# A two-block sequence model on one core: x and the parameter vectors arrive with channels over the partitions

## The chip, the cores and the metric

The kernel runs on one core of one Trainium2 chip. The metric is the device time of one execution in microseconds (us). Three timed runs of the kernel before gave 2650.94, 2653.60 and 2653.69 us, median 2653.6 us. One further execution was recorded by the profiler; its own time is 2655.73 us and its span, first to last instruction, 2653.9 us.

## The reference, cut to what matters

Two blocks follow each other on an array x of 1024 tokens by 1024 channels, all in float32. Only the beginning of the first block and its first residual are touched by the change:

```python
def rms_norm(x, g):
    y = xf * lax.rsqrt(jnp.mean(xf * xf, axis=-1, keepdims=True) + EPS)
    return (y * g.astype(jnp.float32)).astype(x.dtype)

h = rms_norm(x, g_mix[l])
z = jnp.einsum("bsd,de->bse", h, w_in[l]) + b_in[l]
va, ga, xb, gb, sa, sb = jnp.split(z, cuts, axis=-1)
...   # a convolution branch, a gated linear recurrence branch, their mixture m
x = x + jnp.einsum("bsd,de->bse", m, w_o[l])
h = rms_norm(x, g_mlp[l])
f = jnp.square(jax.nn.relu(jnp.einsum("bsd,df->bsf", h, w_1[l])))
x = x + jnp.einsum("bsf,fd->bsd", f, w_2[l])
```

Behind it come the second block (pooling, attention to a memory, a chunked matrix LSTM) and a last norm.

## The kernel before, in words

**Layout.** Inside the kernel every activation has its channels over the 128 partitions and its tokens along the free dimension: 8 tiles of 128 channels by 1024 tokens. A tile is worked on in two halves of 512 tokens ("half 0", "half 1"), and a half of a tile fills one PSUM bank. x itself comes from memory with tokens over the partitions (x_in, 8 tiles of 128 tokens by 1024 channels).

**Products.** A float32 product is made of three matmuls on values split in a high and a low part (three_products, L535 to L537: hi x hi, hi x lo, lo x hi). One weight block is 1024 rows by 128 output columns, 512 KB. For each half, block_product runs over 8 row tiles with three matmuls each, 24 in all, each 512 columns wide. The weight blocks have numbers in the order of use. Each is loaded by SyncE into one of 2 raw buffers, split by ScalarE (whi<-raw, L903) and VectorE (wlo<-raw, L1422) into one of 3 pairs of buffers; a split of block i waits until block i - 3 has been used for both halves ("used"), a load of block i until block i - 2 has been split. `ahead(k)` in an engine's program stands where it does this work up to block k.

**Order.** Every engine has its own program, written out by hand, which it runs strictly in order; points (names such as ("xb", 0, 0, 1)) join them by semaphores. PSUM banks go round in a ring of 8.

**The front.** SyncE loads the identity, four x tiles, block 0, the first group of parameter vectors, four x tiles, block 1, and the other three parameter groups; the 19 parameter vectors come as rows of 128 values. ScalarE squares each token tile with a running sum along the channels (x_squares, L923), takes the root; VectorE scales x by the factor (x_scales, L1464); TensorE transposes x (turn_x, L587) and the parameter rows (turn_rows, L566). Each transposed half tile is split from PSUM with the gain g_mix: high part by ScalarE (L912), low part by VectorE (L1437). TensorE's order is: parameter group 0; x half 0; blocks ("xb", 0, 0) and ("gb", 0, 0) on half 0; x half 1; parameter groups 1 to 3; block ("gb", 0, 1) on half 0; the same three blocks (called FIRST) on half 1, one after the other; then the block ("xb", 0, 1), and so on through the whole projection.

**The later stages that matter.** Three groups of recurrence gates with convolutions on VectorE (57 to some 525 us), then the 31-tap convolution on VectorE beside TensorE's projections (to 914 us), a layer norm, the product w_a_out, and from 1049 us the product with w_o, called "wo": 8 blocks by 2 halves.

**The residual before.** For each half of a "wo" tile, SyncE loads the piece of x with tokens over the partitions (xcols, L464), and TensorE adds it into the same bank by four matmuls of 128 columns against the identity (L678), behind the product's 24. ScalarE copies the bank out as x1 (L1119) and splits the high part for the next product; VectorE makes the low part and the sum of squares.

Of the kernel before, what the change touches and what calls it, by code (L numbers as in the profile page):

```python
# [6 lines left out]
ALU = mybir.AluOpType  # L7
ACT = mybir.ActivationFunctionType

P = 128  # L10
# [109 lines left out]
def build_program(nc, A, out):  # L120
    ctx = ExitStack()
    with ctx:
# [141 lines left out]
        x_rows = A["x"].rearrange("b (t p) d -> p (b t) d", p=P)  # L264
        x_in = sb("x_in", "y", 0, [P, NT, D])
        square_out = sb("square_out", "g", 32 * KB, [P, D])
        rows_in = [sb(f"rows_in{i}", "g", 36 * KB + 512 * i, [P, P]) for i in range(4)]
        row_pieces = [[] for _ in range(4)]
        for name, rows in PARAMS:
            a = A[name]  # L270
            flat_rows = a.rearrange("l (k p) -> (l k) p", p=P) if len(a.shape) == 2 else (
                a.rearrange("(k p) -> k p", p=P) if len(a.shape) == 1 else a.rearrange("l t (k p) -> (l t k) p", p=P))
            done = 0
            while done < rows:
                r = offsets[name] + done
                n = min(rows - done, P - r % P)
                row_pieces[r // P].append((rows_in[r // P][r % P:r % P + n, :], flat_rows[done:done + n, :]))
                done += n
# [35 lines left out]
        xcols = [sb(f"xcols{n}", "g", 64 * KB + 2048 * n, [P, NT // 2, P]) for n in range(2)]  # L314
# [75 lines left out]
        landings = ([f"rows{s}" for s in range(4)] + [f"x{t}" for t in range(NT)] + ["raw0", "raw1"]  # L390
# [9 lines left out]
        def sync(sp):  # L400
# [20 lines left out]
            def load_rows(s):  # L421
                for n, (dst, src) in enumerate(row_pieces[s]):
                    point = [("rows", s)] if n == len(row_pieces[s]) - 1 else []
                    sp.dma_start(dst, src).then_inc(*landed(f"rows{s}", *point))

            def load_x(t):
                sp.dma_start(x_in[:, t, :], x_rows[:, t, :]).then_inc(*landed(f"x{t}", ("x_in", t)))
# [16 lines left out]
            for t in range(NT // 2, NT):  # L444
                load_x(t)
            ahead(0)
            for s in range(1, 4):
                load_rows(s)
# [7 lines left out]
            for j in range(DT):  # L456
                ahead(number["wo", j] + 2)
                for half in range(2):
                    if j:
                        w.wait_ge(*at("x1_sum", j - 1, half))  # L460
# [3 lines left out]
                    sp.dma_start(xcols[half][:], x_rows[:, half * 4:half * 4 + 4, j * P:(j + 1) * P]).then_inc(  # L464
                        *landed(f"xc{half}", ("xcols", j, half)))
# [56 lines left out]
        def tensor(pe):  # L522
# [39 lines left out]
            def turn_rows(s):  # L562
                b = bank("rows", s)
                w.wait_ge(*at("rows", s))
                w.wait_ge(*at("ident"))
                pe.transpose(b[:, 0:P], rows_in[s][:], ident[:]).then_inc(*up("pe_done", ("rows_turned", s)))  # L566

# [13 lines left out]
            def turn_x(half):  # L581
                for j in range(DT):
                    b = bank("x", j, half)
                    for q in range(4):
                        t = half * 4 + q
                        w.wait_ge(*at("normed", t))
                        turned = pe.transpose(b[:, q * P:(q + 1) * P], x_in[:, t, j * P:(j + 1) * P], ident[:])  # L587
                    turned.then_inc(*up("pe_done", ("x", j, half)))
# [13 lines left out]


            turn_rows(0)
            turn_x(0)
            for key in FIRST[:2]:
                block_product(number[key], (*key, 0), h, "h", 0, used=False)
            turn_x(1)
            for s in range(1, 4):
                turn_rows(s)  # L610
            block_product(number[FIRST[2]], (*FIRST[2], 0), h, "h", 0, used=False)
            for key in FIRST:
                block_product(number[key], (*key, 1), h, "h", 1)
# [59 lines left out]
            for j in range(DT):  # L673
                for half in range(2):
                    b = block_product(number["wo", j], ("wo", j, half), mx, "mx", half, stop=False, used=half == 1)
                    w.wait_ge(*at("xcols", j, half))
                    for q in range(4):
                        last = pe.matmul(b[:, q * P:(q + 1) * P], xcols[half][:, q, :], ident[:], start=False, stop=q == 3,  # L678
                                         skip_group_check=True)
                    last.then_inc(*up("pe_done", ("x1_sum", j, half)))  # L680
# [210 lines left out]
        def scalar(act):  # L891
# [27 lines left out]
            def x_squares(half):  # L919
                for t in range(half * 4, half * 4 + 4):  # L920
                    w.wait_ge(*at("x_in", t))
                    w.wait_ge(*now("act_done"))
                    act.activation(square_out[:], x_in[:, t, :], ACT.Square, accum_out=stat[:, t:t + 1]).then_inc(*did(("x_square", t)))  # L923
                root(slice(half * 4, half * 4 + 4), f"x{half}")

            def h_tiles(half):
                for j in range(DT):
                    w.wait_ge(*at("x", j, half))
                    w.wait_ge(*at("par", 0))
                    split_hi(("h_hi", j, half), h[0][j][:, cut(half)], bank("x", j, half)[:], C("g_mix", j))  # L930

            w.wait_ge(*at("ones"))
            act.activation(square_out[:, 0:8], ones[:], ACT.Sqrt).then_inc(*did(("table",)))
# [87 lines left out]

            xb_tile(0, 0, [0])
# [91 lines left out]
            for j in range(DT):  # L1114
                ahead(number["wo", j] + 2)
                for half in range(2):
                    w.wait_ge(*at("x1_sum", j, half))
                    w.wait_ge(*at("mx_lo", j, 0))
                    act.activation(x1[j][:, cut(half)], bank("wo", j, half)[:], ACT.Copy).then_inc(  # L1119
                        *did(("x1", j, half), ("free", "wo", j, half)))  # L1120
                    w.wait_ge(*now("act_done"))
# [16 lines left out]
            for f in range(FC):  # L1138
                for j in range(DT):
# [5 lines left out]
                    for half in range(2):  # L1145
                        t = tmp[half]
                        w.wait_ge(*at("relu", f, j, half))
                        act.activation(t[:], t[:], ACT.Square).then_inc(*did(("relu_square", f, j, half)))  # L1148
                        w.wait_ge(*now("act_done"))
                        w.wait_ge(*(at("w2", f - 1, DT - 1, 1) if f else at("x1_sum", DT - 1, 1)))  # L1150
                        split_hi(("ff_hi", f, j, half), ff[0][j][:, cut(half)], t[:])
# [258 lines left out]
        def vector(dve):  # L1410
# [36 lines left out]
            def turn_rows(s):  # L1447
                block = slice(s * P, (s + 1) * P)
                w.wait_ge(*at("rows_turned", s))
                dve.tensor_copy(par[:, block], bank("rows", s)[:, 0:P]).then_inc(*did(("free", "rows", s)))  # L1450
                own()
                dve.tensor_scalar(parh[:, block], par[:, block], 0.5, None, ALU.mult).then_inc(*did(("par", s)))

# [3 lines left out]
            def x_scales(half):  # L1457
                columns = slice(half * 4, half * 4 + 4)
                w.wait_ge(*at("x_square", half * 4 + 3))
                mean(columns, f"x{half}")  # L1460
                inverse(columns, f"x{half}")
                own()
                for t in range(half * 4, half * 4 + 4):
                    dve.tensor_scalar(x_in[:, t, :], x_in[:, t, :], stat[:, t:t + 1], None, ALU.mult).then_inc(*did(("normed", t)))  # L1464

            def h_tiles(half):
                for j in range(DT):
                    w.wait_ge(*at("h_hi", j, half))
                    scaled_lo(("h_lo", j, half), h[1][j][:, cut(half)], bank("x", j, half)[:], C("g_mix", j), h[0][j][:, cut(half)],
                              ("free", "x", j, half))  # L1470

            x_scales(0)
            turn_rows(0)
            ahead(0)
            h_tiles(0)
            ahead(1)
            dve.memset(xb_in[:, 0:PAD_B], 0.0).then_inc(*did(("xb_pad",)))
            x_scales(1)
            ahead(2)
            h_tiles(1)  # L1480
            for s in range(1, 4):
                turn_rows(s)
# [624 lines left out]
        def gpsimd(pool):  # L2107
            w = Once(pool)
            w.wait_ge(*at("x", DT - 1, 1))
# [40 lines left out]
```

## Time and profile before

| | |
|---|---|
| median of three runs | 2653.6 us |
| the profiled execution's own time | 2655.73 us |
| its span | 2653.9 us |
| TensorE, matmuls | 2493.1 us busy, 94% |
| VectorE | 1413.2 us busy, 53% |
| ScalarE | 810.3 us busy, 31% |
| DMA, mean share of the 16 engines | 17.0% |
| mean granted TensorE clock | 0.971 of 2.4 GHz |

How to read it: the busy times are those of one execution on the chip. PE is TensorE's matmuls, PEld its weight loads (they overlap), DVE is VectorE, ACT ScalarE, POOL GpSimd, SP SyncE. A float32 matmul that is not split leaves two records. Matmuls are pipelined, so the distance from one start to the next tells more than the duration of one. PEclk is the granted clock as a share of 2.4 GHz; the first record of it is a rise at 19.9 us, and windows ahead of that show 1.00 without one.

### The profile page before, as it was taken

How to read it: one execution, taken by the hardware profiler on the slowest of the kernel's cores; microseconds unless marked ns; L12 is line 12 of the kernel's file. 1: busy time of each engine (PE TensorE's matmuls, PEld its weight loads, DVE VectorE, ACT ScalarE, POOL GpSimd, SP SyncE). 2: the span in 40 equal slices, each digit the busy share in tenths (PEclk: the TensorE clock that was granted, in tenths of full speed). 3: DMA queues.
4: the chain of work that ended last, by engine and by line, in shares of the span. 5: the costliest groups of instructions: out<-in, count | busy, mean ns of one | idle time of the engine just before them, and what ended most of it. 6: DMA issues, size and time to landing. Idle time of an engine off the chain costs nothing.

```text
span 2653.9 us, 26240 instructions
## 1 busy us (share of the span) xinstructions
PE 2493.1 (94%) x11144; PEld 2015.3 (76%) x11144; DVE 1413.2 (53%) x1699; ACT 810.3 (31%) x1202; POOL 2.8 (0%) x7
## 2 busy tenths in 40 slices
PE   8999999999999469999999999999789999999678
PEld 6686867788888148888888888887678777878577
DVE  5665665598899974243232232334665333631365
ACT  5435252512121152332022130232332231221354
POOL 0000000000000000000000000000000000000000
PEclk9999999999999789999999999999799999999889
DMA  4010202011111002211111111121111111111401
GB/s 133 27 56 27 64 12 70 20 55 48 48 48 48 16 15 61 83 49 55 48 48 48 48 48 53 46 69 40 50 46 56 38 33 48 40 48 55 128 22 59
DMA packets 224951, 133.15 MB, mean 50 GB/s; under 512 B 12730, under 2 KB 220858, under 8 KB 224834
## 3 DMA queue, kind: packets, MB, share of 16 engines
q1 hardware_dynamic: 224834, 131.47, 17.0%
q8 instruction: 88, 1.44, 0.2%
q14 instruction: 29, 0.24, 0.0%
HBM read 125.12 MB, written 6.32 MB: 50 GB/s over the span
## 4 chain that ended last, share of the span: by engine, by line
PE 81%; DVE 12%; ACT 4%; issue 1%; DMA 1%; SPq 1%; ACTq 0%; DVEq 0%
PE bank L535 24%; PE bank L537 24%; PE bank L536 24%; DVE uc L1559 4%; PE bank L599 4%; DVE sa L1559 2%; DVE wlo L1422 1%; PE bank L569 1%; DVE u_in L1559 1%; PE bank L770 1%; PE bank L786 1%; PE bank L678 1%; DVE uc L1676 0%; DVE tmp L1799 0%; PE bank L875 0%
## 5 line engine op out<-in xcount | busy, mean ns | idle before, releaser
L535 PE MATMUL bank<-h_hi,whi 128*128 128x512 f32 x2000 | 787.3, 394 | 3.6 <-issue 3.3
L537 PE MATMUL bank<-h_hi,wlo 128*128 128x512 f32 x2000 | 780.7, 390 | 0.0
L536 PE MATMUL bank<-h_lo,whi 128*128 128x512 f32 x2000 | 780.4, 390 | 0.0
L535 PEld LDWEIGHTS bank<-h_hi,whi 128*128 128x128 f32 x2000 | 376.7, 188 | 84.3 <-issue 5.6
L536 PEld LDWEIGHTS bank<-h_lo,whi 128*128 128x128 f32 x2000 | 376.7, 188 | 80.3 <-issue 2.9
L537 PEld LDWEIGHTS bank<-h_hi,wlo 128*128 128x128 f32 x2000 | 376.5, 188 | 78.7
L903 ACT ACTIVATE whi<-raw 128x1024 fp32r<-128x1024 f32 (+2 forms) x212 | 216.8, 1023 | 448.6 <-PE bank L537 446.6
L1422 DVE TENSOR_TENSOR wlo<-raw,whi 128x1024 fp32r<-128x1024 f32 (+2 forms) x212 | 251.4, 1186 | 163.5 <-ACT whi L903 161.8
L1559 DVE SCALAR_TENSOR_TENSOR uc<-u_in,par,uc 128x1024 f32<-128x1024 f32 x163 | 205.5, 1281 | 1.1
L537 PE MATMUL bank<-ff_hi,wlo 128*128 128x512 f32 x512 | 199.4, 389 | 0.0
L536 PE MATMUL bank<-ff_lo,whi 128*128 128x512 f32 x512 | 199.4, 389 | 0.0
L535 PE MATMUL bank<-ff_hi,whi 128*128 128x512 f32 x512 | 199.4, 389 | 0.0
L1770 DVE TENSOR_TENSOR x<-x,bank 128x512 f32<-128x512 f32 x64 | 44.0, 688 | 229.8 <-PE bank L537 229.8
L536 PEld LDWEIGHTS bank<-ff_lo,whi 128*128 128x128 f32 x512 | 96.2, 188 | 19.9
L535 PEld LDWEIGHTS bank<-ff_hi,whi 128*128 128x128 f32 x512 | 96.1, 188 | 19.9
L537 PEld LDWEIGHTS bank<-ff_hi,wlo 128*128 128x128 f32 x512 | 96.1, 188 | 19.9
L1148 ACT ACTIVATE tmp<-tmp 128x512 f32<-128x512 f32 x64 | 40.5, 632 | 227.4 <-DVE tmp L1759 227.4
L1759 DVE SCALAR_TENSOR_TENSOR tmp<-bank,factor 128x512 f32<-128x512 f32 x64 | 44.2, 691 | 115.9 <-PE bank L537 115.9
L599 PE MATMUL bank<-v,gate_w 128*128 128x512 f32 x224 | 97.5, 592 | 0.0
L1434 DVE TENSOR_TENSOR ff_lo<-tmp,ff_hi 128x512 fp32r<-128x512 f32 x64 | 44.3, 693 | 87.2 <-ACT ff_hi L912 87.2
L599 PEld LDWEIGHTS bank<-v,gate_w 128*128 128x128 f32 x224 | 42.6, 190 | 50.4 <-issue 48.3
L537 PE MATMUL bank<-vg_hi,wlo 128*128 128x512 f32 x192 | 75.9, 395 | 0.0
(341 smaller groups left out, 3075.5 us busy)
## 6 DMA issues: line engine op xcount, KB each, us to landing
raw<-in_w_in SPq DMA_DIRECT2D x92, 512.0 KB, 3.6
raw<-in_w SPq DMA_DIRECT2D x64, 512.0 KB, 3.8
raw<-in_w_b_out SPq DMA_DIRECT2D x16, 384.0 KB, 3.0
raw<-in_w_out SPq DMA_DIRECT2D x11, 512.0 KB, 3.4
x_in<-in_x SPq DMA_DIRECT2D x8, 512.0 KB, 5.5
raw<-in_w_a_out SPq DMA_DIRECT2D x8, 512.0 KB, 3.8
raw<-in_w_o SPq DMA_DIRECT2D x8, 512.0 KB, 3.5
xcols<-in_x SPq DMA_DIRECT2D x16, 256.0 KB, 2.8
```

The source lines that it names most:

```text
L535: pe.matmul(target, lh, rh, start=start, stop=False, skip_group_check=True)
L536: pe.matmul(target, lh, rl, start=False, stop=False, skip_group_check=True)
L537: last = pe.matmul(target, ll, rh, start=False, stop=stop and point is not None, skip_group_check=True)
L569: pe.matmul(b[:], ones_sq[:], data, start=j == 0, stop=j == DT - 1, skip_group_check=True).then_inc(*up("pe_done", point))
L599: last = pe.matmul(b[:], gate_w[n][:, PAIRS.index((a, c)), :], v[a][:, cut(half)], start=m == 0, stop=m == len(rows_) - 1)
L903: act.activation(hi, raw_, ACT.Copy).then_inc(*up("w_hi_done", ("w_hi", i)))
L1148: act.activation(t[:], t[:], ACT.Square).then_inc(*did(("relu_square", f, j, half)))
L1422: dve.tensor_tensor(lo, raw_, hi.bitcast(F32), ALU.subtract).then_inc(*up("w_lo_done", ("w", i)))
L1434: dve.tensor_tensor(lo, value, hi.bitcast(F32), ALU.subtract).then_inc(*did(name, *more))
L1559: dve.scalar_tensor_tensor(to, source, weight, to, ALU.mult, ALU.add).then_inc(*did(*point))
L1759: dve.scalar_tensor_tensor(t[:], b[:], 0.0, factor[:, cut(half)], ALU.max, ALU.mult).then_inc(*did(("relu", f, j, half), ("free", "w1", f, ...
L1770: dve.tensor_tensor(x1[j][:, cut(half)], x1[j][:, cut(half)], b[:], ALU.add).then_inc(*did(("x1_add", f, j, half), ("free", "w2", f, j, ha ...
```

## The change

- The host passes x transposed (x_t, channels by tokens) and all parameter vectors in one array of 128 by 512 (par). x_in is loaded as 8 pieces of two channel tiles by 512 tokens; par by one DMA. The loads of rows, their transposes and the transposes of x are gone.
- The mean square of a token is now a sum over partitions. ScalarE squares each channel half tile into one of four buffers x_sq; TensorE multiplies it, 128 tokens at a time, as the stationary operand with one column of ones and adds over the 8 tiles in one bank (x_sums); VectorE, ScalarE and VectorE make the factor from 4 columns; TensorE spreads it over the partitions (x_spread, 4 matmuls of 128 columns). VectorE multiplies x by gain and factor into one of four buffers x_z, ScalarE makes the high part, VectorE the low part, one tile behind.
- Blocks of FIRST are run abreast, tile by tile, in two or three banks (blocks_together): the first two on half 0, the third on half 0, all three on half 1.
- VectorE splits blocks 0 and 1 ahead of the h tiles.
- In "wo" the identity matmuls and ScalarE's copy are gone. VectorE adds the bank and xcols, which is now loaded with channels over the partitions, into x1.
- GpSimd's clearing of the gate weights no longer waits for the transposes.

```diff
-            for t in range(NT // 2):
-                load_x(t)
-            ahead(-1)
-            load_rows(0)
...
+            for j in range(0, DT, 2):
+                load_x(0, j)
             sp.dma_start(ident[:], A["ident"]).then_inc(*landed("ident", ("ident",)))
+            sp.dma_start(par[:], A["par"]).then_inc(*landed("par", ("par_in",)))
             ahead(0)
+            for j in range(0, DT, 2):
+                load_x(1, j)
...
+            def x_sums(half):
+                b = bank("x_sums", half)
+                for j in range(DT):
+                    w.wait_ge(*at("x_square", j, half))
+                    for q in range(4):
+                        last = pe.matmul(b[:, q:q + 1], x_sq[j % 4][:, q * P:(q + 1) * P], ones[:, 0:1], start=(j, q) == (0, 0), stop=j == DT - 1,
+                                         skip_group_check=True)
+                    last.then_inc(*up("pe_done", ("x_sum", j, half)))
+
+            def x_spread(half):
+                w.wait_ge(*at("ident"))
+                w.wait_ge(*at(f"x{half}"))
+                spread(0, half, "x_scale")
+
+            def blocks_together(keys, half):
+                together = [bank(*key, half) for key in keys]
+                for n in range(DT):
+                    w.wait_ge(*at("h_lo", n, half))
+                    for key, b in zip(keys, together):
...
+                        point = [(*key, half)] + ([("used", k)] if half else []) if n == DT - 1 else None
+                        three_products(...)
...
+            x_sums(0)
+            x_spread(0)
+            blocks_together(FIRST[:2], 0)
+            x_sums(1)
+            x_spread(1)
+            blocks_together(FIRST[2:], 0)
+            blocks_together(FIRST, 1)
             for t in range(1, GT):
                 block(("xb", 0, t), h, "h")
...
-                    b = block_product(number["wo", j], ("wo", j, half), mx, "mx", half, stop=False, used=half == 1)
-                    w.wait_ge(*at("xcols", j, half))
-                    for q in range(4):
-                        last = pe.matmul(b[:, q * P:(q + 1) * P], xcols[half][:, q, :], ident[:], start=False, stop=q == 3,
-                                         skip_group_check=True)
+                    block_product(number["wo", j], ("wo", j, half), mx, "mx", half, used=half == 1)
...
 # ScalarE
+                for j in range(DT):
+                    w.wait_ge(*at("x_in", j // 2 * 2, half))
+                    if half or j >= 4:
+                        w.wait_ge(*(at("x_sum", j - 4, half) if j >= 4 else at("x_sum", j + 4, 0)))
+                    act.activation(x_sq[j % 4][:], x_in[:, j, cut(half)], ACT.Square).then_inc(*did(("x_square", j, half)))
...
             x_squares(0)
             ahead(0)
+            root(slice(0, 4), "x0")
+            ahead(1)
             h_tiles(0)
-            ahead(1)
             x_squares(1)
+            root(slice(4, 8), "x1")
             ahead(2)
 # VectorE
+            w.wait_ge(*at("par_in"))
+            dve.tensor_scalar(parh[:], par[:], 0.5, None, ALU.mult).then_inc(*did(("par",)))
+            x_factors(0)
             ahead(0)
+            ahead(1)
             h_tiles(0)
...
+            x_factors(1)
             ahead(2)
             h_tiles(1)
...
+                    w.wait_ge(*at("wo", j, half))
+                    w.wait_ge(*at("xcols", j, half))
+                    dve.tensor_tensor(x1[j][:, cut(half)], bank("wo", j, half)[:], xcols[half][:], ALU.add).then_inc(
+                        *did(("x1", j, half), ("free", "wo", j, half)))
                     w.wait_ge(*at("h2_hi", j, half))
```

## Rows read from the trace of the kernel before

**Rows 1.** The page, part 1: busy us, share of the span, instructions.

```profile
PE 2493.1 (94%) x11144; PEld 2015.3 (76%) x11144; DVE 1413.2 (53%) x1699; ACT 810.3 (31%) x1202; POOL 2.8 (0%) x7
```

**Rows 2.** Windows: stretch and its length, busy us (instructions) of PE, PEld, DVE, ACT, POOL, PEclk, DMA.

```profile
57.00:877.00 820.00, 820.00 (x3374) 633.92 (x3373) 610.83 (x620) 270.50 (x321) 0.00 (x0) 1.00 0.15 44
...
600.00:700.00 100.00, 100.00 (x443) 82.87 (x442) 85.86 (x80) 20.83 (x27) 0.00 (x0) 1.00 0.18 53
```

**Rows 3.** Timeline of the front: start us, us, what, [idle before and its releaser].

```profile
5.34 1.06 ACT L923 ACTIVATE square_out<-x_in 128x1024 f32<-128x1024 f32 x1 [3.11 <-DMA x_in<-in_x]
10.75 0.17 DVE L1441 TENSOR_SCALAR stat<-stat 128x4 f32<-128x4 f32 x1 [9.72 <-ACT square_out L923]
11.41 0.75 DVE L1464 TENSOR_SCALAR x_in<-x_in,stat 128x1024 f32<-128x1024 f32 x1
12.37 0.47 PE L566 MATMUL bank<-ident,rows_in 128*128 128x128 f32 x1 [12.37 <-DMA rows_in<-in_lam]
14.21 6.15 PE L587 MATMUL bank<-ident,x_in 128*128 128x128 f32 x29 [0.19 <-DVE x_in L1464]
20.11 0.47 PE L535 MATMUL bank<-h_hi,whi 128*128 128x512 f32 x1
31.11 3.65 PE L587 MATMUL bank<-ident,x_in 128*128 128x128 f32 x32
35.39 0.50 PE L535 MATMUL bank<-h_hi,whi 128*128 128x512 f32 x1 [0.29 <-DVE h_lo L1437]
57.28 0.39 PE L535 MATMUL bank<-h_hi,whi 128*128 128x512 f32 x1
```

**Rows 4.** ScalarE's drain of "wo" (first and last start us), and the identity matmuls' timeline.

```profile
L1119 ACT ACTIVATE x<-bank x16: 597/597/597, 1056.1 to 1151.3; 128x512 f32<-128x512 f32 x16
...
1055.05 1.05 PE L678 MATMUL bank<-ident,xcols 128*128 128x128 f32 x8
```

**Rows 5.** An add from PSUM (the page, part 5), and one half's work in "wo".

```profile
L1770 DVE TENSOR_TENSOR x<-x,bank 128x512 f32<-128x512 f32 x64 | 44.0, 688 | 229.8 <-PE bank L537 229.8
...
1139.27 0.72 ACT L912 ACTIVATE h_hi<-x,par 128x512 fp32r<-128x512 f32 x1
1140.03 0.75 DVE L1437 SCALAR_TENSOR_TENSOR h_lo<-x,par,h_hi 128x512 fp32r<-128x512 f32 x1 [4.99 <-ACT h_hi L912]
```

**Rows 6.** One-column matmuls: windows of L687 and what follows it; timeline of L849.

```profile
1862.90:1869.70 6.80, 6.80 (x32) 6.80 (x33) 0.00 (x0) 0.00 (x0) 0.00 (x0) 0.50 0.00 0
1869.70:1873.30 3.60, 3.60 (x18) 3.60 (x19) 2.13 (x9) 1.37 (x3) 0.00 (x0) 0.50 0.02 5
...
2497.46 0.95 PE L849 MATMUL bank<-ones,kts 128*128 128x1 f32 x8
```

**Rows 7.** A square, a scaled z, its high and low part (128x512 each), later in the kernel.

```profile
L1148 ACT ACTIVATE tmp<-tmp 128x512 f32<-128x512 f32 x64 | 40.5, 632 | 227.4 <-DVE tmp L1759 227.4
...
1895.66 0.63 ACT L912 ACTIVATE h_hi<-tmp 128x512 fp32r<-128x512 f32 x1 [1.42 <-DVE tmp L1799]
1896.33 0.69 DVE L1434 TENSOR_TENSOR h_lo<-tmp,h_hi 128x512 fp32r<-128x512 f32 x1 [0.69 <-ACT h_hi L912]
1896.93 0.74 DVE L1799 SCALAR_TENSOR_TENSOR tmp<-x,small,bank 128x512 f32<-128x512 f32 x1
```

**Rows 8.** Timeline of block 3's split, and the work behind it on VectorE.

```profile
47.19 1.05 ACT L903 ACTIVATE whi<-raw 128x1024 fp32r<-128x1024 f32 x1
48.27 1.23 DVE L1422 TENSOR_TENSOR wlo<-raw,whi 128x1024 fp32r<-128x1024 f32 x1 [8.92 <-ACT whi L903]
49.41 0.81 DVE L1495 TENSOR_SCALAR v<-xb_in,par 128x1024 f32<-128x1024 f32 x1
```

**Rows 9.** Products after idle time: timeline at 944 us, and windows around 1900 us.

```profile
945.13 0.63 PE L536 MATMUL bank<-un_lo,whi 128*128 128x512 f32 x1
945.55 0.63 PE L537 MATMUL bank<-un_hi,wlo 128*128 128x512 f32 x1
...
1907.00:1910.90 3.90, 0.60 (x4) 0.54 (x4) 2.92 (x4) 1.58 (x3) 0.00 (x0) 1.00 0.00 0
```

More of the change, by code:

```diff
@@ L261, in weight_views @@
                     wlo[k % 3][:, 0:n].rearrange("p (k c) -> p k c", k=kt))
[L264 to L278, printed above, removed]
+        x_t = A["x_t"].rearrange("(j p) t -> p j t", p=P)
+        x_in = sb("x_in", "y", 0, [P, DT, SEQ])
+        x_sq = [sb(f"x_sq{n}", "g", 48 * KB + 2048 * n, [P, HALF]) for n in range(4)]
+        x_z = [sb(f"x_z{n}", "g", 56 * KB + 2048 * n, [P, HALF]) for n in range(4)]
         h = pair("h", "h", 0, DT)
@@ L313, in build_program @@
         x1 = [sb(f"x1_{j}", "y", 4096 * j, [P, SEQ]) for j in range(DT)]
-        xcols = [sb(f"xcols{n}", "g", 64 * KB + 2048 * n, [P, NT // 2, P]) for n in range(2)]
+        xcols = [sb(f"xcols{n}", "g", 64 * KB + 2048 * n, [P, HALF]) for n in range(2)]
         squares = [sb(f"squares{n}", "g", 68 * KB + 2048 * n, [P, HALF]) for n in range(2)]
@@ L388, in build_program @@
         add_keys = {"yb": GT, "ob": NH, "oc": NH}
-        landings = ([f"rows{s}" for s in range(4)] + [f"x{t}" for t in range(NT)] + ["raw0", "raw1"]
+        landings = (["par"] + [f"x{half}_{j}" for half in range(2) for j in range(0, DT, 2)] + ["raw0", "raw1"]
                     + ["ident", "mask", "gate0", "gate1", "xc0", "xc1", "mem", "bias", "rcnt", "row_out", "mp", "last", "gain"]
@@ L419, in ahead, with load_x @@
                         sp.dma_start(view[:, :, c0:c1], src).then_inc(*landed(f"raw{i % 2}", *point))
[L421 to L427, printed above, removed]
+            def load_x(half, j):
+                sp.dma_start(x_in[:, j:j + 2, cut(half)], x_t[:, j:j + 2, cut(half)]).then_inc(*landed(f"x{half}_{j}", ("x_in", j, half)))
             def load_gates(g):
@@ L459, in sync @@
                     if j:
-                        w.wait_ge(*at("x1_sum", j - 1, half))
+                        w.wait_ge(*at("x1", j - 1, half))
                     else:
@@ L463, in sync @@
                         w.wait_ge(*at("mixed", DT - 1, 1))
[L464 removed]
+                    sp.dma_start(xcols[half][:], x_t[:, j, cut(half)]).then_inc(
                         *landed(f"xc{half}", ("xcols", j, half)))
@@ L919, in x_squares @@
             def x_squares(half):
[L920 to L924, printed above, removed]
+                for j in range(DT):
[3 more added lines that the diff above has]
+                    act.activation(x_sq[j % 4][:], x_in[:, j, cut(half)], ACT.Square).then_inc(*did(("x_square", j, half)))
             def h_tiles(half):
                 for j in range(DT):
-                    w.wait_ge(*at("x", j, half))
-                    w.wait_ge(*at("par", 0))
-                    split_hi(("h_hi", j, half), h[0][j][:, cut(half)], bank("x", j, half)[:], C("g_mix", j))
+                    w.wait_ge(*at("x_z", j, half))
+                    split_hi(("h_hi", j, half), h[0][j][:, cut(half)], x_z[j % 4][:])
             w.wait_ge(*at("ones"))
-            act.activation(square_out[:, 0:8], ones[:], ACT.Sqrt).then_inc(*did(("table",)))
+            act.activation(small[:, 0:8], ones[:], ACT.Sqrt).then_inc(*did(("table",)))
             x_squares(0)
             ahead(0)
+            root(slice(0, 4), "x0")
+            ahead(1)
             h_tiles(0)
-            ahead(1)
             x_squares(1)
+            root(slice(4, 8), "x1")
             ahead(2)
@@ L1116, in scalar @@
                 for half in range(2):
[L1117 to L1121, printed above, removed]
+                    w.wait_ge(*at("x1", j, half))
                     w.wait_ge(*at("ya", DT - 1, 1))
@@ L1445, in inverse @@
                 dve.reciprocal(stat[:, columns], stat[:, columns]).then_inc(*did((name,)))
[L1447 to L1452, printed above, removed]
             dve.memset(ones[:], 1.0).then_inc(*did())
@@ L1456, in vector, with x_factors @@
             dve.memset(ones_sq[:], 1.0).then_inc(*did(("ones",)))
-            def x_scales(half):
+            def x_factors(half):
                 columns = slice(half * 4, half * 4 + 4)
-                w.wait_ge(*at("x_square", half * 4 + 3))
-                mean(columns, f"x{half}")
+                w.wait_ge(*at("x_sum", DT - 1, half))
+                dve.tensor_scalar(stat[:, columns], bank("x_sums", half)[:, 0:4], 1.0 / D, EPS, ALU.mult, ALU.add).then_inc(
+                    *did((f"x{half}_mean",), ("free", "x_sums", half)))
@@ L1461, in x_scales @@
                 inverse(columns, f"x{half}")
[L1462 to L1470, printed above, removed]
@@ L1472, in vector, with h_tiles @@
-            x_scales(0)
-            turn_rows(0)
+            def h_tiles(half, follow=()):
+                b = bank("x_scale", half)
+                w.wait_ge(*at("x_scale", half))
+                for j in range(DT + 1):
+                    if j < DT:
+                        if half or j >= 4:
+                            w.wait_ge(*(at("h_lo", j - 4, half) if j >= 4 else at("h_lo", j + 4, 0)))
+                        dve.scalar_tensor_tensor(x_z[j % 4][:], x_in[:, j, cut(half)], C("g_mix", j), b[:], ALU.mult, ALU.mult).then_inc(
+                            *did(("x_z", j, half), *([("free", "x_scale", half)] if j == DT - 1 else [])))
+                    if j:
+                        w.wait_ge(*at("h_hi", j - 1, half))
+                        split_lo(("h_lo", j - 1, half), h[1][j - 1][:, cut(half)], x_z[(j - 1) % 4][:], h[0][j - 1][:, cut(half)])
@@ L2141 @@
                  "rcnt": rcnt}
+    inputs = {name: np.asarray(a, np.float32) for name, a in inputs.items()}
+    columns = [inputs.pop(name).reshape(-1, P) for name, _ in PARAMS]
+    constants["par"] = np.concatenate(columns).T
+    constants["x_t"] = inputs.pop("x").reshape(SEQ, D).T
     for name, a in [*inputs.items(), *constants.items()]:
```

38 lines of the change are left out of this document (6 added, 32 removed).

## The prediction, made before the changed kernel was run

> **What bounds the kernel now.** I read the page's busy times first, then windows over the stages, then the timeline of the first 60 us and of the residual at 1055 us. On the page the reader sees TensorE at 94% of the span and VectorE at 53% [rows 1]. The windows show TensorE full from 57 to 877 us, with VectorE at 74% over all of it and 86% from 600 to 700 us, its convolution [rows 2]. So VectorE still has gaps there, where it waits for TensorE's blocks, so a delay of TensorE in the first 57 us is carried on into VectorE's late stretch and to the end, one for one. In the first 57 us the timeline shows three stretches of products: the first from 20.11 us, ended by 31.1 us, the rest from 35.39 us; the block ("xb", 0, 1) starts at 57.28 us, and from there TensorE is never short of work [rows 3]. That start is my first mark. The second is the output product of the mixer, "wo": its 16 drains start from 1056.1 to 1151.3 us, so a half tile takes (1151.3 - 1056.1) / 15 = 6.35 us, all of it TensorE's [rows 4].
>
> **The residual ("wo").** Four float32 matmuls against the identity stand behind each product. They leave 8 records, 8 x 0.112 = 0.9 us [rows 4]. The product itself is 24 matmuls at 0.227 us (in the front 96 such matmuls go from 35.39 to 57.28, the first of them slow [rows 3]), 5.44 us. Sum 6.35, as measured. Taken away 16 times: 16 x 0.91 = 14.5 us gained. In their place VectorE adds x from PSUM, nearest row 0.69 us for the same shape [rows 5], and ScalarE no longer copies. VectorE's part of a half is then 0.69, a wait of 0.72 for ScalarE's split, 0.75 for the lo part, some 0.69 for the square total [rows 5], and a weight split of 1.22 every second half: under 4.1 us of 5.44. Queued behind the new wait are only that half's own operations. At the end of the stage the up-projection needs the last half 5.44 us after it was produced; add, split and lo part take 2.2 us. So the edit costs nothing elsewhere; if VectorE's part did become the bound it would be worth the lost cover, at most 14.5 us. The x tiles are asked for one tile ahead (10.9 us) as before.
>
> **The front: what goes.** 64 transposes of x: 32 of them before 20.1 us at about 0.21 us, 32 after 31.11 us in 3.65 us; the parameter transposes, 8 scalings of x on VectorE (0.75 us) and 22 small loads. None of the loads ended a wait but the first.
>
> **The front: the sums of squares.** With channels on the partitions the mean is over partitions, so x_sums issues 8 x 4 float32 matmuls of one column for each half. The same kind stands in the trace (L687, 16 matmuls, 32 records): 32 records in 6.8 us, 0.213 us each at a granted clock of 0.50, that is 1.2 GHz [rows 6]. At 2.4 GHz the same kind took 8 records in 0.95 us with the drain, 0.112 us each [rows 6]. So a half is 64 records: 64 x 0.213 = 13.6 us at 1.2 GHz, 64 x 0.112 = 7.2 us at 2.4 GHz. These are the ends; I take 13.6 us for half 0, since TensorE comes from idle.
> The Trainium skill ("TensorE: Matmul & The Clock Gate", section "LDWEIGHTS (loading the stationary operand)") gives a weight load as its columns over 1.2 GHz, 107 ns for 128, with no word of the array's clock. By it a half of sums would be 64 x 0.107 = 6.8 us whichever clock is granted. The trace agrees at the high clock (0.112) and not at the low one (0.213), so the sum does not use it.
> Does this work raise the clock? The window from 1862.9 to 1869.7 us is nothing but such matmuls, TensorE busy all of it, and the clock stayed 0.50; the window behind it, 3.6 us of 256-column products, still shows 0.50, and only then it rose [rows 6]. I take it that it does not raise it.
>
> **Half 0, in us.** First x tile used 5.34 [rows 3]; ScalarE squares a 512 piece in 0.63 [rows 7]; TensorE starts the sums at about 5.7, is slower (1.7 a tile) than squares and loads, and ends at 19.4. Mean, root, reciprocal: 0.25 wait and 0.66 (10.75 to 11.41 [rows 3]): 20.2. VectorE now splits blocks 0 and 1 first, 2 x 1.15 (48.27 to 49.41 [rows 8]): 22.5; the spread over TensorE, 8 x 0.213 = 1.7, is beside it. Then per tile z on VectorE (0.74), hi on ScalarE (0.63), lo on VectorE (0.69) [rows 7]; as lo runs one tile behind z, VectorE's pace is 0.67 + 0.60 = 1.27, and the first lo is ready at 24.6. Products start at 24.7 instead of 20.11. Two blocks abreast need 6 x 0.227 = 1.36 per tile, just over VectorE's pace: 10.9 us. But TensorE has idled about 2.7 us behind the slow spread and starts at 1.2 GHz. Other starts from idle show the price: 512 columns take 0.43 instead of 0.23 [rows 9], and the clock is back after 3.6 us of products (1869.7 to 1873.3) or 7.5 us (12.4 to 19.9, transposes) [rows 3, 6]. Lost is 1 - 0.227/0.427 = 47% of that time, 1.7 to 3.5; I take 5 us, 2.4. Ends: 24.7 + 10.9 + 2.4 = 38.0. Before: 31.1.
>
> **Half 1.** The sums wait in TensorE's queue behind those products. After a pause the granted clock held for some 3.9 us and then fell (1907.0 to 1910.9) [rows 9]: 3.5 us of sums at 0.112 (31 records), 33 at 0.213: 10.5 us (ends 7.2 and 13.6). 48.5. Factor, 0.9: 49.4. Block 2's split follows on ScalarE and VectorE (1.05 and 1.22, ScalarE's part beginning with the reciprocal): 51.6; the spread is beside it. Before, TensorE was here at 35.39. Then 96 matmuls x 0.227 = 21.8, as before, plus 2.4 for the low clock: 75.8. VectorE's tiles, done by 65, don't hold this up.
>
> **A wait that is added.** The three blocks run abreast to the last tile, so all three weight buffers come free only at the end; block 3's hi split waits for the first of them. Behind it: ScalarE copies xb half 1 (0.59), splits hi (1.05), VectorE lo (1.23) [rows 8], beginning 1.2 us before TensorE ends: ("xb", 0, 1) starts 1.8 us late, at 77.6. Before, block 3 was split at 47.19 to 49.5, 8 us ahead. VectorE's convolution and GELU stand 7 us later against TensorE than before; its idle time before the gates takes that up.
>
> **Sum.** Front 77.6 - 57.3 = 20.3 lost, residual 14.5 gained: +5.8 us. On the profiled execution's own 2655.7 us that is 2661.5; that execution lay 2.1 us above the median of the runs, 2653.6, so the prediction is 2659.4 us. The parameter load of 256 KB, POOL's clearing moved to the start and the halved parameters (one VectorE operation) lie in VectorE's idle time before 19 us; without that cover they would be about 1 us.
>
> **Rivals.**
> (a) One-column matmuls do raise and hold the clock, ends on the faster side. Sums of half 0: 35 records at 0.213, then 29 at 0.112, end 16.4; factor 17.2, splits 19.5, products 21.7 to 32.6 at full clock; sums 7.2 to 39.8; 40.6; block 2 at 42.7; 64.5; 66.3. Front 9.0 lost, net -5.5, 2648.1 us. For it: TensorE's queue is full all the time. Against it: [rows 6]. It decides from where the front loses less than 14.5 us. Chance 0.20.
> By the skill's load time the front would come out close to this too.
> (b) The low clock lasts longer everywhere: sums of half 1 all at 0.213 (+3.1), each restart 7.5 us (+1.1 twice): net +11.1, 2664.7 us. For it: the start at 12.4 us took that long [rows 3]. Against it: the products at 1869.7 us took 3.6 [rows 6]. Chance 0.12.
> (c) The residual gives nothing, because VectorE's add becomes late: +20.3, 2673.9 us. Against it: 1.3 us and more to spare in each half. Chance 0.03. That a loss before 57 us is absorbed by VectorE's late stretch, net -14.5, has 0.02.
> The forecast has 0.63, its own range 2656 to 2663.
>
> **How the numbers follow.** A measurement of this kernel can tell about 0.2%, 5.3 us: slower begins at 2658.9, just under the forecast, faster at 2648.3. Slower: 0.58 of the forecast's 0.63, (b), (c): 0.52. Faster: a third of (a), and 0.02: 0.09. The rest, 0.39, is no change. The range 2648 to 2667 takes in (a) and (b).
>
> **What would show it.** "wo" drains every 5.44 us, its identity matmuls gone: else the 14.5 is wrong. x_sums of half 0 in 13.6 us at 0.213, of half 1 in 7.2 to 13.6; first product at 24.7; first matmuls at 0.43; ("xb", 0, 1) at 77.6 with TensorE idle 1.8 us ahead of it. If the sums run at 0.112, (a) holds. If TensorE has gaps after 80 us that it had not, a consumer is late and the sum lacks a term.

## The result, and the profile of the changed kernel

The changed kernel takes 2657.28 us against 2652.61 us before (medians of 20 runs each, taken side by side): ratio 1.0019, 95% interval 1.0013 to 1.0026. It is 4.7 us, 0.2%, slower. Forecast were 5.8 us more and 2659.4 us. One of the changed kernel's 20 runs was a slow one, 13480.1 us; nothing here explains it, the interval is worked out without it, and it does not move the median.

The first view is the timeline of the front of the changed kernel. Line numbers have moved: L561 is x_sums, L551 the spread, L516 to L518 the three products, L886 and L1403 the high and the low part of a weight block.

```profile
4.20 1.15 ACT L907 ACTIVATE x_sq<-x_in 128x512 f32<-128x512 f32 x2 [1.96 <-DMA x_in<-in_x_t]
4.88 13.82 PE L561 MATMUL bank<-ones,x_sq 128*128 128x1 f32 x64 [4.88 <-ACT x_sq L907]
19.16 0.18 DVE L1426 RECIPROCAL stat<-stat 128x4 f32<-128x4 f32 x1 [0.27 <-ACT stat L899]
19.26 2.33 DVE L1403 TENSOR_TENSOR wlo<-raw,whi 128x1024 fp32r<-128x1024 f32 x2
21.57 1.41 DVE L1445 SCALAR_TENSOR_TENSOR x_z<-x_in,par,bank 128x512 f32<-128x512 f32 x2
23.77 0.79 PE L516 MATMUL bank<-h_hi,whi 128*128 128x512 f32 x1 [2.23 <-DVE h_lo L1415]
...
36.27 9.71 PE L561 MATMUL bank<-ones,x_sq 128*128 128x1 f32 x64
48.67 0.79 PE L516 MATMUL bank<-h_hi,whi 128*128 128x512 f32 x1
...
72.05 1.23 DVE L1403 TENSOR_TENSOR wlo<-raw,whi 128x1024 fp32r<-128x1024 f32 x1 [12.77 <-ACT whi L886]
73.42 0.47 PE L516 MATMUL bank<-h_hi,whi 128*128 128x512 f32 x1 [1.72 <-DVE wlo L1403]
```

The reader sees the two blocks of 64 records that replaced the transposes, 13.8 and 9.7 us long, and that VectorE has two weight splits to do behind the first before it can touch a tile. Against [rows 3] the first product comes at 23.77 instead of 20.11 us, the second stretch at 48.67 instead of 35.39, and the block ("xb", 0, 1) at 73.42 instead of 57.28: 16.1 us lost.

Between half 1's sums and the product at 48.67 lie 2.7 us, in which TensorE has only the spread to do:

```profile
46.32 1.04 ACT L886 ACTIVATE whi<-raw 128x1024 fp32r<-128x1024 f32 x1
46.68 2.08 PE L551 MATMUL bank<-ident,stat 128*128 128x128 f32 x8 [0.71 <-DVE stat L1426]
47.39 1.23 DVE L1403 TENSOR_TENSOR wlo<-raw,whi 128x1024 fp32r<-128x1024 f32 x1 [0.77 <-ACT whi L886]
```

That product, block ("gb", 0, 1) on half 0, needs nothing of half 1. It stands behind half 1's sums and spread in TensorE's program, and it waits for the split of its weights, which ScalarE and VectorE have behind half 1's root and factor, though the block's load was issued at 20.5 us. No run put the split or the product ahead, so what this order costs is not shown.

The second view is the residual stage: VectorE's add from the bank, with the start of the first and the last of the 16.

```profile
L1700 DVE TENSOR_TENSOR x<-bank,xcols x16: 691/692/692, 1070.8 to 1152.4; 128x512 f32<-128x512 f32 x16
```

(1152.4 - 1070.8) / 15 = 5.44 us for a half, where [rows 4] has 6.35: 16 x 0.91 = 14.5 us gained. VectorE waits for TensorE ahead of every add, 0.5 and 3.2 us ahead of the first two and then 1.3 and 2.6 us in turn, so it has room:

```profile
1147.00 0.69 DVE L1700 TENSOR_TENSOR x<-bank,xcols 128x512 f32<-128x512 f32 x1 [1.26 <-PE bank L518]
1152.44 0.69 DVE L1700 TENSOR_TENSOR x<-bank,xcols 128x512 f32<-128x512 f32 x1 [2.60 <-PE bank L518]
```

The third view is TensorE's waits from 57 to 900 us in the changed kernel (us in total, times, longest). There are two: the weight split, and 0.6 us in the gates of the recurrence, for VectorE. The kernel before has none in this stretch.

```profile
PE bank L516 <- DVE wlo L1403: 1.7, 1, 1.7
PE bank L590 <- DVE lru L1496: 0.6, 1, 0.6
```

The last view is windows of the changed kernel over half 1's sums and the products behind them (columns as in [rows 2]; the last but two is the granted clock).

```profile
36.30:40.60 4.30, 4.30 (x41) 4.30 (x39) 0.00 (x0) 2.52 (x4) 0.00 (x0) 1.00 0.00 0
40.60:46.00 5.40, 5.37 (x26) 5.29 (x25) 0.00 (x0) 0.00 (x0) 0.00 (x0) 0.50 0.00 0
46.70:50.80 4.10, 4.10 (x13) 3.50 (x14) 3.19 (x4) 3.01 (x5) 0.00 (x0) 0.50 0.20 56
```

The clock fell 4.3 us into the one-column matmuls although TensorE was busy with them all the time (about 0.11 us each ahead of the fall, 0.21 behind it), and the spread and the first products ran at 1.2 GHz.

In the two profiled executions themselves the spans differ by 0.7 us only (2653.9 and 2654.6). The front is 16.1 us late, TensorE's end before the layer norm 17.1 (877.3 and 894.3), and "wo" gives 14.5 back. Another 1.5 us comes back between 944 and 1049 us, from where the low clock of 1.2 GHz lies in these two executions: behind TensorE's last wait for the normed tiles it lasted 5.8 us before (980.15 to 985.9) and 2.4 us in the changed kernel (997.24 to 999.7). The 0.4 us that is left I can't place.

### The profile page after: what moved, and what is told of

Its sections match the earlier page's. It is cut to its first block, busy times and chain, and to the rows that moved or that the text cites. A ratio compares the mean times of both kernels' runs of the same rounds, so it can differ in the third digit from the quotient of the medians.

```text
span 2654.6 us, 26124 instructions
## 1 busy us (share of the span) xinstructions
PE 2497.7 (94%) x11092; PEld 2017.9 (76%) x11092; DVE 1426.8 (54%) x1716; ACT 800.7 (30%) x1186; POOL 2.8 (0%) x7
## 4 chain that ended last, share of the span: by engine, by line
PE 79%; DVE 14%; ACT 5%; issue 1%; DMA 1%; SPq 1%; ACTq 0%; DVEq 0%
PE bank L516 24%; PE bank L518 24%; PE bank L517 24%; DVE uc L1537 4%; PE bank L590 3%; DVE sa L1537 2%; DVE wlo L1403 1%; PE bank L561 1%; PE bank L544 1%; DVE u_in L1537 1%; PE bank L753 1%; PE bank L769 1%; ACT whi L886 0%; DVE tmp L1781 0%; DVE uc L1654 0%
## 5 line engine op out<-in xcount | busy, mean ns | idle before, releaser
L516 PE MATMUL bank<-h_hi,whi 128*128 128x512 f32 x2000 | 786.8, 393 | 6.7 <-issue 2.7
L518 PE MATMUL bank<-h_hi,wlo 128*128 128x512 f32 x2000 | 779.6, 390 | 0.0
L516 PEld LDWEIGHTS bank<-h_hi,whi 128*128 128x128 f32 x2000 | 376.5, 188 | 88.3 <-issue 5.0
L518 PEld LDWEIGHTS bank<-h_hi,wlo 128*128 128x128 f32 x2000 | 376.3, 188 | 78.7
L886 ACT ACTIVATE whi<-raw 128x1024 fp32r<-128x1024 f32 (+2 forms) x212 | 216.7, 1022 | 446.2 <-PE bank L518 444.6
L1403 DVE TENSOR_TENSOR wlo<-raw,whi 128x1024 fp32r<-128x1024 f32 (+2 forms) x212 | 251.2, 1185 | 162.6 <-ACT whi L886 161.1
L518 PE MATMUL bank<-ff_hi,wlo 128*128 128x512 f32 x512 | 199.2, 389 | 0.0
L516 PE MATMUL bank<-ff_hi,whi 128*128 128x512 f32 x512 | 199.2, 389 | 0.0
L516 PEld LDWEIGHTS bank<-ff_hi,whi 128*128 128x128 f32 x512 | 96.1, 188 | 19.9
L518 PEld LDWEIGHTS bank<-ff_hi,wlo 128*128 128x128 f32 x512 | 96.1, 188 | 19.9
L518 PE MATMUL bank<-vg_hi,wlo 128*128 128x512 f32 x192 | 75.8, 395 | 0.0
```

Source lines behind the costliest of these rows:

```text
L516: pe.matmul(target, lh, rh, start=start, stop=False, skip_group_check=True)
L518: last = pe.matmul(target, ll, rh, start=False, stop=stop and point is not None, skip_group_check=True)
L886: act.activation(hi, raw_, ACT.Copy).then_inc(*up("w_hi_done", ("w_hi", i)))
L1403: dve.tensor_tensor(lo, raw_, hi.bitcast(F32), ALU.subtract).then_inc(*up("w_lo_done", ("w", i)))
```

## Experiments

All times are medians. The kernel before, run beside them, took 2652.36 us for e1 to e4 and 2652.14 us for e5 to e8, where it had 2652.61 us beside the changed kernel; "under the changed kernel" is the distance to its 2657.28 us. Each version has one profiled execution. The mark is the start of the block ("xb", 0, 1). The theory: the front costs 16 to 20 us, through the records of x_sums, the low clock and the waits behind them, and the residual gives 14.5; rivals are named in the expectations.

**e1, the residual alone.** The kernel before, with x_t as a second input and the diff's edits of "wo" only.

```diff
-                    for q in range(4):
-                        last = pe.matmul(b[:, q * P:(q + 1) * P], xcols[half][:, q, :], ident[:], start=False, stop=q == 3,
+                    dve.tensor_tensor(x1[j][:, cut(half)], bank("wo", j, half)[:], xcols[half][:], ALU.add).then_inc(
```

> The front of the kernel before, with only the residual of the change: x comes a second time with channels over the partitions, VectorE adds it in wo, the 64 identity matmuls are gone. Theory (the front costs 16 to 20 us, the residual gives 14.5): wo drains every 5.44 us instead of 6.35, the block (xb, 0, 1) starts at 57.3 us as before, the time is 14.5 us under before, about 2638 us. Rival (the residual's gain is small or given back behind it by VectorE's add, and the front is nearly free): within 5 us of before.

Measured: 2638.53 us, ratio 0.9945 (0.9933 to 0.9958), 13.8 us faster. VectorE's adds start from 1053.0 to 1134.6 us, 5.44 us apart. The rival is out.

```profile
L1714 DVE TENSOR_TENSOR x<-bank,xcols x16: 691/692/692, 1053.0 to 1134.6; 128x512 f32<-128x512 f32 x16
```

**e2, the front alone.** The changed kernel with the old residual (x also comes in rows).

```diff
-                    block_product(number["wo", j], ("wo", j, half), mx, "mx", half, used=half == 1)
+                    b = block_product(number["wo", j], ("wo", j, half), mx, "mx", half, stop=False, used=half == 1)
+                    w.wait_ge(*at("xcols", j, half))
+                    for q in range(4):
+                        last = pe.matmul(b[:, q * P:(q + 1) * P], xcols[half][:, q, :], ident[:], start=False, stop=q == 3,
```

> The changed front with the residual of the kernel before. Theory: (xb, 0, 1) starts at 73 to 77 us, the time is 17 to 20 us over before, about 2671 us, and together with the residual-only kernel it adds up to the change. Rival (a delay of the front is taken up by VectorE's late stretch): under 8 us over before.

Measured: 2672.02 us, ratio 1.0073 (1.0061 to 1.0086), 19.7 us slower. The mark in its profiled execution:

```profile
74.23 0.47 PE L517 MATMUL bank<-h_hi,whi 128*128 128x512 f32 x1 [1.72 <-DVE wlo L1413]
```

19.7 lost and 13.8 gained make 5.9, measured together 4.9 over this before: the parts add up to within the scatter of the runs, and nothing of the loss is absorbed later.

The mark of one front is not the same in every execution. e1 has the front of the kernel before, yet reaches the mark at 55.80 us and not at 57.28. The last 29 records of its transposes of half 0 begin at the same time but take 4.77 us instead of the 6.15 of [rows 3], and its first product comes at 18.65 instead of 20.11 us:

```profile
14.12 4.77 PE L588 MATMUL bank<-ident,x_in 128*128 128x128 f32 x29 [0.19 <-DVE x_in L1456]
18.65 0.47 PE L536 MATMUL bank<-h_hi,whi 128*128 128x512 f32 x1
```

The clock rose sooner there: 14 of these records stand in the 2.9 us to 17.0 us, 15 in the 1.4 us from 17.2. e2 has the changed front and is 0.8 us behind the changed kernel at the mark. So the front costs 16.1 us at the mark by one pair of executions and 74.23 - 55.80 = 18.4 by the other, and ahead of the layer norm, where VectorE's convolution ends, 17.1 (913.86 and 930.95 us) and 19.3 (912.38 and 931.72). The second pair fits the 19.7 us of the timed runs.

**e3, wider sums.** The same 64 weight loads and records, with 128 columns of ones as the moving operand.

```diff
-                        last = pe.matmul(b[:, q:q + 1], x_sq[j % 4][:, q * P:(q + 1) * P], ones[:, 0:1], ...
+                        last = pe.matmul(b[:, q * P:(q + 1) * P], x_sq[j % 4][:, q * P:(q + 1) * P], ones_sq[:], ...
```

> The changed kernel, but each of the 64 matmuls of x_sums has 128 columns of ones instead of one; as many weight loads and records. Theory (one-column matmuls do not raise the clock and let it fall): with 128 columns the granted clock rises within the sums of half 0, which end at about 14.5 us instead of 18.7, and holds through those of half 1, 7.2 us instead of 9.7; (xb, 0, 1) starts 6 to 8 us earlier, the time is about 2650 us. Rival (the clock depends only on TensorE having work, whatever its width, or the wider matmuls cost time themselves): sums as long as with one column or longer, time unchanged at 2657 or above.

Measured: 2649.08 us, ratio to before 0.9987 (0.9978 to 0.9996): 8.2 us under the changed kernel. Timeline and windows:

```profile
5.32 9.15 PE L561 MATMUL bank<-ones_sq,x_sq 128*128 128x128 f32 x64 [5.32 <-ACT x_sq L907]
32.01 7.30 PE L561 MATMUL bank<-ones_sq,x_sq 128*128 128x128 f32 x64
65.82 0.47 PE L516 MATMUL bank<-h_hi,whi 128*128 128x512 f32 x1 [1.72 <-DVE wlo L1403]
```

```profile
5.30:9.00 3.70, 3.68 (x17) 3.68 (x18) 0.00 (x0) 1.64 (x3) 0.00 (x0) 1.00 1.00 341
9.10:14.50 5.40, 5.37 (x49) 5.18 (x47) 0.43 (x1) 3.36 (x5) 0.00 (x0) 1.00 1.08 330
32.00:39.30 7.30, 7.30 (x65) 7.11 (x63) 0.00 (x0) 2.52 (x4) 0.00 (x0) 1.00 0.00 0
```

17 records in the first 3.7 us (0.21 each), 49 in the next 5.4 (0.11): the clock's first recorded rise lies at 9.0 us, against 26.9 in the changed kernel, and half 1's sums run at 2.4 GHz to their end. More columns cost nothing and give 7.6 us at the mark. That the sums of half 0 ran without a rise is no accident of one execution: those of e2 and e5, also of one column, took 13.82 and 13.81 us. So the clock makes the changed front slow as much as the number of records does. The Trainium skill ("TensorE: Matmul & The Clock Gate", section "LDWEIGHTS (loading the stationary operand)") puts a load at its columns over 1.2 in ns, 107 for 128 columns. By that rule both versions would have, as an estimate, sums of 64 x 0.107 = 6.8 us; the runs agree at 2.4 GHz (7.30 / 64 = 0.114) and not at 1.2 GHz (13.82 / 64 = 0.216), and there the measurement decides.

**e4, fewer records.** VectorE adds the eight squared tiles, TensorE sums one.

```diff
+                for j in range(1, DT):
+                    w.wait_ge(*at("x_square", j, half))
+                    own()
+                    dve.tensor_tensor(x_z[3][:], left[:], x_sq[j % 4][:], ALU.add).then_inc(...)
...
+                w.wait_ge(*at("x_acc", DT - 1, half))
+                for q in range(4):
+                    last = pe.matmul(b[:, q:q + 1], x_z[3][:, q * P:(q + 1) * P], ones[:, 0:1], start=q == 0, stop=True,
```

> The changed kernel, but VectorE adds the eight squared tiles of a half (7 adds of 0.69 us) and TensorE sums only the result over the partitions: 4 matmuls instead of 32 for each half. Theory (the 64 records of x_sums set the front): first product at 18.4 us instead of 23.8, first product after half 1's sums at 36 instead of 48.7, (xb, 0, 1) at 60.5 instead of 73.4, time about 2644.5 us. Rival (the loads of x, the splits ahead of the tiles or VectorE's pace set the front): less than 4 us gained.

Measured: 2649.94 us, ratio 0.9991 (0.9982 to 1.0000), 7.3 us under the changed kernel where 12.8 were expected. The timeline shows why:

```profile
10.05 0.43 DVE L1457 TENSOR_SCALAR parh<-par 128x512 f32<-128x512 f32 x1 [9.02 <-DMA par<-in_par]
10.58 0.69 DVE L1436 TENSOR_TENSOR x_z<-x_sq,x_sq 128x512 f32<-128x512 f32 x1
...
16.11 1.87 PE L560 MATMUL bank<-ones,x_z 128*128 128x1 f32 x8 [16.11 <-DVE x_z L1436]
...
66.36 0.47 PE L516 MATMUL bank<-h_hi,whi 128*128 128x512 f32 x1 [1.72 <-DVE wlo L1402]
```

The mark is at 66.36 us where 60.5 was expected. VectorE's first instruction waits for the parameters, and the adds stand behind it. In the changed kernel that wait is covered by the long sums; I had counted it as covered here too. My size was wrong, the direction right.

**e5, in turn.** The changed kernel; on half 1 the three blocks one after the other.

```diff
-            blocks_together(FIRST, 1)
+            for key in FIRST:
+                block_product(number[key], (*key, 1), h, "h", 1)
```

> The changed kernel, but on half 1 the three first blocks run one after the other instead of abreast (on half 0 as changed). Theory (abreast, all three weight buffers come free only at the end, and block 3's split is then waited for): the 1.7 us in which TensorE waits for VectorE's weight split before (xb, 0, 1) go to 0, that block starts at 71.7 us instead of 73.4, time 1.7 us under the changed kernel, which is near what can be told. Rival (in turn, TensorE outruns VectorE's low parts of half 1 and waits there): as much or more idle time between 50 and 62 us, the mark unchanged.

Measured: 2654.72 us, ratio to before 1.0010 (1.0001 to 1.0019), 2.6 us under the changed kernel; the intervals of the two ratios overlap, so the time alone does not tell. The timeline does: TensorE has no idle time from 50 us to the mark, so the rival is out too. The mark is at 71.89 us where 71.7 was expected, and the 0.6 us in the gates are gone as well.

```profile
71.66 0.39 PE L518 MATMUL bank<-h_hi,wlo 128*128 128x512 f32 x1
71.89 0.39 PE L516 MATMUL bank<-h_hi,whi 128*128 128x512 f32 x1
```

**e6, e4 with the halving behind the factor.**

```diff
-            w.wait_ge(*at("par_in"))
-            dve.tensor_scalar(parh[:], par[:], 0.5, None, ALU.mult).then_inc(*did(("par",)))
             x_factors(0)
+            w.wait_ge(*at("par_in"))
+            dve.tensor_scalar(parh[:], par[:], 0.5, None, ALU.mult).then_inc(*did(("par",)))
```

> The vector-sums kernel, in which the seven adds of half 0 began only at 10.4 us, because VectorE's first instruction, the halving of the parameters, waits for their load; here that instruction stands behind the factor of half 0. Theory (head of VectorE's queue): the adds follow the squares, TensorE's short sum starts at about 12.1 instead of 16.1 us, the first product at 19.5 instead of 23.1, (xb, 0, 1) at 62.8 instead of 66.4, time about 2646.3 us. Rival (loads of x or VectorE's add pace set it): sum start later than 15 us, less than 1.5 us gained.

Measured: 2644.19 us, ratio 0.9970 (0.9958 to 0.9981), 5.8 us under e4. The short sum now starts at 11.8 us, the first product at 18.96, the mark at 60.66 where 62.8 was expected.

```profile
11.76 1.87 PE L560 MATMUL bank<-ones,x_z 128*128 128x1 f32 x8 [11.76 <-DVE x_z L1436]
...
18.96 0.80 PE L516 MATMUL bank<-h_hi,whi 128*128 128x512 f32 x1 [2.49 <-DVE h_lo L1414]
...
60.66 0.47 PE L516 MATMUL bank<-h_hi,whi 128*128 128x512 f32 x1 [1.72 <-DVE wlo L1402]
```

Not all of it is the order on VectorE. Against e4 the first product is 4.1 us earlier (23.05 and 18.96), and so is the first product behind half 1's sums (40.98 and 36.88). The other 1.6 us of the 5.7 at the mark is the clock: these products ran at 1.2 GHz in e4's execution, 0.43 us apart, and at 2.4 GHz in e6's. First e4, then e6:

```profile
40.98 0.63 PE L516 MATMUL bank<-h_hi,whi 128*128 128x512 f32 x1 [0.83 <-DVE wlo L1402]
41.41 0.63 PE L517 MATMUL bank<-h_lo,whi 128*128 128x512 f32 x1
...
36.88 0.50 PE L516 MATMUL bank<-h_hi,whi 128*128 128x512 f32 x1 [0.83 <-DVE wlo L1402]
37.22 0.39 PE L517 MATMUL bank<-h_lo,whi 128*128 128x512 f32 x1
```

**e7, e6 with half 1 in turn** (both diffs above).

> Both together: vector sums, halving of the parameters behind the factor, and the three blocks of half 1 in turn. The best of the changed front by this theory: (xb, 0, 1) at 61.1 us, time about 2644.6 us, still 6 us over the residual-only kernel (2638.5), whose front reaches that mark at 57.3.

Measured: 2641.50 us, ratio 0.9963 (0.9950 to 0.9977); mark at 59.29 us. That is 3.1 us less than expected, 2.1 of them by which e6 lies under its own forecast too, and 3.0 us over the residual-only kernel instead of 6. The order of the blocks gave 1.4 us at the mark against e6, where 1.7 were said.

**e8, the residual alone and the parameters in one array.** To e1, the load of par in place of the 22 loads of rows; turn_rows is gone from TensorE and VectorE.

```diff
-            load_rows(0)
+            sp.dma_start(par[:], A["par"]).then_inc(*landed("par", ("par_in",)))
...
-            turn_rows(0)
             turn_x(0)
```

> The residual-only kernel, and the parameters come as one array with channels over the partitions: 22 loads, four transposes and eight small VectorE operations fall away; x is still transposed on TensorE. Theory: none of these ended a wait but three transposes and a bank between the halves, so (xb, 0, 1) starts 0.5 to 1 us earlier than with the old front, and the time is 2638 us, the same as residual-only within the noise. Rival (the earlier landing of x tiles 4 to 7 and of the weights moves the second half forward): 3 us or more earlier.

Measured: 2636.20 us, ratio 0.9939 (0.9927 to 0.9952), the fastest version of all, 16 us under before. Its mark, and under it that of e1:

```profile
54.85 0.39 PE L516 MATMUL bank<-h_hi,whi 128*128 128x512 f32 x1
```

```profile
55.80 0.39 PE L536 MATMUL bank<-h_hi,whi 128*128 128x512 f32 x1
```

0.95 us between them is the theory's, and at the place that it named: the two are level at the start of half 1's transposes (29.58 and 29.65 us), and the distance is there at the next product, where the transposes of the parameter rows are gone. First e8, then e1:

```profile
32.99 0.47 PE L516 MATMUL bank<-h_hi,whi 128*128 128x512 f32 x1
...
33.93 0.50 PE L536 MATMUL bank<-h_hi,whi 128*128 128x512 f32 x1 [0.29 <-DVE h_lo L1429]
```

The 2.3 us between the medians of e8 and e1 are within what five runs of each tell. So the half of the change that pays is the residual, with a little from the parameters; the transposes of x are cheaper than what took their place in every form tried (marks 54.9 and 55.8 against 59.3 for the best new front).

## Why the prediction was right

It was right in direction and size, and its mechanism is the one that the traces show. That the size came out so near is in part luck: the terms of the front came to 4.2 us too much at the mark (77.6 said, 73.42 seen), and most of what made up for it lay outside the sum, in where it starts from and behind the mark. By its steps:

- *The residual*, 14.5 us: 5.44 us a half as said; alone it gave 13.8 (e1). No wait of VectorE or later work ate it, and the 1.3 us that VectorE had to spare are there.
- *Half 0's sums*, 13.6 us at 0.213: 13.8 us. The first product was said for 24.7 and came at 23.77; nearly all of the difference is the start, 4.88 instead of 5.7. The first piece of x, 512 KB as before, is now asked for ahead of the identity, at 0.73 us instead of 1.18, and is squared from 4.20 us instead of 5.34.
- *The low clock behind them*: said 5 us, seen 3.1 (23.8 to 26.9), so the products end at 36.3 instead of 38.0. This varies: with the same front e2's lasted 4.0 us (24.2 to 28.2).
- *Half 1's sums*, 10.5 us with a fall after 3.5: 9.7 us with a fall after 4.3. The 3.5 was carried over from [rows 9], a stretch in which TensorE was busy for 0.6 of 3.9 us, to one in which it was busy throughout. No row joined the two, so its fit is luck. Then 2.1 us at the low clock (48.7 to 50.8), not 5.
- *The added wait*, 1.8 us: 1.72, and e5 took it away by its cause.
- *The loads*: "None of the loads ended a wait but the first" is not what [rows 3] show, where TensorE's first instruction waits for rows_in until 12.37 us. It cost nothing: e8, without these loads, starts its transposes of x at 12.24 us, waits for VectorE's scaled tiles, and is level with e1 from then on (14.14 and 14.12 us).
- *The sum*, front 20.3: 16.1 and 18.4 at the mark in the two pairs of profiled executions, 19.7 in the timed runs of e2. Part of the difference is the execution of the kernel before in [rows 3], which the sum starts from: e1, with the same front, reaches the mark 1.5 us earlier, since the clock rose sooner within its transposes. The runs scatter in the same way: 19 of the changed kernel's 20 runs spread over 8.0 us (2654.06 to 2662.07) and e5's eleven over 8.0, both with the fall inside half 1's sums, while e3's eleven, without it, spread over 3.6 and the kernel before over 4.3. That the scatter comes from where the clock rises and falls is argued, not shown.
- *VectorE's later place is taken up by its idle time*: not quite. 0.6 us of a new wait in the gates, and with it 1.0 us in all between the mark's 16.1 and the 17.1 us ahead of the layer norm. The sum has this term at nothing; 0.4 us of it stay unplaced.
- *The rivals*: (a) is out, as the clock did not rise in 13.8 us of one-column matmuls and fell during them; e3 is what (a) would have been, and (a) forecast 2648.1 where e3 has 2649.1. (b) is out in the trace: half 1's sums took 9.7 us and not 13.6, and the low clock behind the two starts 3.1 and 2.1 us and not 7.5. (c) is out by e1, and that VectorE's late stretch absorbs the loss is out by e2.

## What to carry to other kernels

A layout change that removes transposes has to be charged with the reduction that it moves onto the partitions. For each half, 32 transposes leave 32 records here (x32 for half 1 in [rows 3]) and 32 matmuls with a column of ones leave 64. They took TensorE 13.8 and 9.7 us, where the transposes took 7.5 (12.64 to 20.11 us, waits included) and 3.7, and they leave the engine at 1.2 GHz for the products behind them. Before, the squares and scalings of half 1 also lay beside TensorE's products (21.95 to 30.24 us); now its sums stand between them. Look for the part of such a change that stands in a stage bound by TensorE (the residual's identity matmuls) and take it alone. And a first instruction that waits for a load is free only as long as everything behind it on its queue is later than the load (4.1 us at the first product, e6 against e4).

## What the runs showed of the hardware

- A float32 matmul with 128 stationary columns leaves two records, and each took the same time with 1 moving column as with 128: at 2.4 GHz 0.112 and 0.114 us, at 1.2 GHz 0.216 (changed kernel) and 0.22 (e3, 17 records in 3.7 us). So the wider form cost TensorE nothing here.
- TensorE busy with one-column matmuls ran at 1.2 GHz through all of 13.8 us. The first record of the clock in that execution is the rise at 26.9 us, so this is read from the 0.216 us of a record, the pace of the 0.50 window in [rows 6]. With 2.4 GHz at the start it lost it after 4.3 us (changed kernel) and 4.4 us (e5). With 128 columns in the same instructions the clock rose 3.7 us after their start and held for the 7.3 us of half 1.
- Where the clock rises differs between executions of the same front: the 29 records of [rows 3] took 6.15 us, those of e1 4.77.
